# A two-layer trunk with expert retrieval: U and V rows of an expert gathered as one 8 KB row

## The reference, cut to what matters

```python
def peer(h, w_query, sub_keys, expert_u, expert_v):     # per block of 128 tokens
    qry = (x_blk @ w_query).reshape(T, 8, 2, 128)
    scores = einsum('thpd,hpnd->thpn', qry, sub_keys)   # 8 heads, 2 halves, 128 sub-keys
    top_s, top_i = top_k(scores, 16)
    ...                                                 # 16 x 16 sums, best 16 -> idx, gate
    gate = softmax(best_s)
    u = expert_u[idx]                                   # 128 picks per token, 1024 values each
    act = gelu(einsum('thkd,td->thk', u, x_blk))
    vsel = expert_v[idx]
    return einsum('thk,thkd->td', gate * act, vsel)
```

## Time and profile before

| | before |
|---|---|
| timed runs, median | 1703.7 us (1703.4 to 1704.94) |
| profiled execution, span (its own time) | 1706.2 us |
| PE busy | 1410.3 us, 83% |
| VectorE (DVE) busy | 965.0 us, 57% |
| ScalarE (ACT) busy | 379.5 us, 22% |
| POOL busy | 1095.4 us, 64% |
| moved by DMA | 619.36 MB, mean 363 GB/s |
| mean granted TensorE clock | 0.956 |

### The profile page before, as it was taken

The page is one execution under the profiler, slowest core; times in us unless marked ns, Lnnn a source line. Parts: engine busy times, 40 slices in busy tenths (PEclk is TensorE's granted clock), DMA queues, the critical chain, the costliest instruction groups (busy, mean ns, idle before and its releaser), DMA issues.

```text
span 1706.2 us, 14289 instructions
## 1 busy us (share of the span) xinstructions
PE 1410.3 (83%) x4185; PEld 672.0 (39%) x4185; DVE 965.0 (57%) x2457; ACT 379.5 (22%) x958; POOL 1095.4 (64%) x1044
## 2 busy tenths in 40 slices
PE   7999789877767898889997699888998667676777
PEld 6555555532222343334652244343663222222223
DVE  3126866758863533564557566585468657444441
ACT  4222211211221221442111221352212112111111
POOL 2003777777877776677667777677757666666663
PEclk9999899999997999989999999999999988999998
DMA  9318999999999999999999999999999999999996
GB/s 340 119 54 308 321 351 368 355 350 405 336 360 405 409 402 403 406 409 399 405 403 409 409 379 402 404 409 405 405 406 382 374 376 365 367 372 370 378 371 234
DMA packets 184836, 619.36 MB, mean 363 GB/s; under 512 B 18420, under 2 KB 18456, under 8 KB 184760
## 3 DMA queue, kind: packets, MB, share of 16 engines
q0 software_dynamic: 151184, 551.68, 83.8%
q1 hardware_dynamic: 33200, 66.72, 10.5%
q10 hardware_dynamic: 376, 0.05, 0.0%
HBM read 617.34 MB, written 1.05 MB: 362 GB/s over the span
## 4 chain that ended last, share of the span: by engine, by line
PE 42%; DMA 20%; POOL 16%; issue 14%; DVE 3%; another core or an unknown queue 3%; ACT 1%; ACTq 0%; SPq 0%; DVEq 0%; POOLq 0%
PE banks L540 24%; POOL arena L301 10%; DMA arena<-in_peer_v_dram,hnT 10%; PE banks L420 5%; POOL raw L301 4%; DMA work<-in_peer_v_dram,hnT 4%; PE banks L564 3%; PE banks L513 3%; DMA raw<-in_peer_u_dram,hnT 3%; DMA arena<-in_peer_w_query_dram 2%; PE banks L683 2%; POOL work L301 2%; PE banks L398 2%; DMA arena<-in_peer_u_dram,hnT 1%
## 5 line engine op out<-in xcount | busy, mean ns | idle before, releaser
L540 PE MATMUL banks<-arena,hnT 128*128 128x512 f32 x1536 | 754.0, 621 | 161.2 <-DMA arena<-in_peer_v_dram,hnT 95.2
L301 POOL DMA_INDIRECT arena<-in_peer_v_dram,hnT x384 | 401.2, 1045 | 236.6 <-issue 97.3
L540 PEld LDWEIGHTS banks<-arena,hnT 128*128 128x128 f32 x1536 | 279.3, 196 | 561.8 <-issue 524.5
L301 POOL DMA_INDIRECT raw<-in_peer_u_dram,hnT x256 | 271.3, 1060 | 214.7 <-DVE hnT L1508 125.3
L1394 DVE CUSTOM_DVE_ANT_0 arena<-arena,hrows 128x1024 f32<-128x1024 f32 x192 | 234.1, 1223 | 184.9 <-DMA arena<-in_peer_u_dram,hnT 144.6
L1394 DVE CUSTOM_DVE_ANT_0 raw<-raw,hrows 128x1024 f32<-128x1024 f32 x192 | 234.5, 1223 | 162.3 <-DMA raw<-in_peer_u_dram,hnT 121.6
L301 POOL DMA_INDIRECT arena<-in_peer_u_dram,hnT x256 | 269.3, 1052 | 81.9 <-issue 77.4
L540 PE MATMUL banks<-work,hnT 128*128 128x512 f32 x512 | 262.1, 639 | 61.8 <-DMA work<-in_peer_v_dram,hnT 38.7
L901 ACT ACTIVATE hnT<-ident,hnT 128x128 f32<-128x128 f32 x512 | 171.1, 392 | 282.1 <-issue 108.2
L301 POOL DMA_INDIRECT work<-in_peer_v_dram,hnT x128 | 144.5, 1129 | 52.8 <-issue 34.8
L540 PEld LDWEIGHTS banks<-work,hnT 128*128 128x128 f32 x512 | 92.6, 200 | 189.3 <-issue 180.2
(11 more groups left out here) (214 smaller groups left out, 960.2 us busy)
## 6 DMA issues: line engine op xcount, KB each, us to landing
arena<-in_diff_w_in_dram SPq DMA_DIRECT2D x24, 1024.0 KB
arena<-in_peer_w_query_dram SPq DMA_DIRECT2D x16, 1024.0 KB
arena<-in_gla_w_in_dram POOLq DMA_DIRECT2D x5, 2048.0 KB, 24.5
arena<-in_peer_w_query_dram SPq DMA_DIRECT2D x4, 2048.0 KB, 9.1
arena<-in_diff_w_out_dram SPq DMA_DIRECT2D x8, 1024.0 KB
arena<-in_peer_v_dram,hnT POOLq DMA_INDIRECT x384
work<-in_gla_w_out_dram POOLq DMA_DIRECT2D x2, 2048.0 KB, 40.2
raw<-in_peer_u_dram,hnT POOLq DMA_INDIRECT x256
```

What stands on the lines that cost most here:

```text
L301: pool.indirect_dma_start(rows(n), None, table.rearrange("l e d -> (l e) d"), bass.IndirectOffsetOnAxis(ap=places[:, o:o + 1].bitcast(u32) ...
L540: last = nc.tensor.matmul(bank(2 * (tile % NT) + half), diags[:, n % BUFS * P:(n % BUFS + 1) * P], v_rows(n)[:, half * 512:(half + 1) * 51 ...
```

## The change

U and V of each layer are laid side by side as `peer_uv` (rows of 8 KB), so one gather brings both rows of a pick. The 16 buffers of 4 KB become 8 "pair" buffers of 8 KB for the first 128 picks and 9 afterwards (`homes`). A buffer is reused when the sum of its last pick is done (`BEFORE`, `v_used`). The lag of 16 picks is gone, and layer 1 begins 14 ticks earlier. GELU, weights and diagonals of a group are made together on ScalarE, in groups of 2 picks, and of 4 during the attention of layer 1 (`groups`); the weights, formerly one VectorE instruction for 8 picks, are now one ScalarE instruction for each pick. The sub-keys come as `peer_keys_t`, already turned, so that the transposes and their copies go. In the diff below the long index expressions of ScalarE's operands are shortened to names.

```diff
-GRP = 8
-BUFS = 8
+DIAGS = 8
-BASE = (148, 276)
-FINAL = 430
+BASE = (134, 262)
+FINAL = 414
+AHEAD = 7
+TICKS = ROWS + LANDED + 4
-ADD_T, HN2_T = (11, 15), 17
-QUERY_T, QUERY_TICKS = {3: 20, 4: 32, 5: 44, 6: 56, 7: 68}, 10
+ADD_T, HN2_T = (8, 10), 12
+QUERY_T, QUERY_TICKS = {2: 10, 3: 22, 4: 38, 5: 56, 6: 74, 7: 90}, 14
...
+def groups():
+    out, n = [], 0
+    while n < ROWS:
+        narrow = all(not b + ATT_T - 2 <= n + LANDED < b + NORM_O + 2 for b in BASE)
+        size = 2 if narrow or n % 4 else 4
+        out.append((n, size))
+        n += size
+    return out
+GROUPS = groups()
+SUM_T = [first + size + LANDED + j for first, size in GROUPS for j in range(size)]
...
+ROW = 2 * D
+EARLY = ("raw0", "raw1", 6144, 4096, "work0", "work1", "work2", "work3")
+LATE = (8192, 10240, 12288, 14336, 20480, "raw0", "raw1", 6144, 4096)
...
@@ sync
-            sp.wait_ge(S("aT_done"), NT)
-            sp.dma_start(keys..., peer_sub_keys[0].rearrange("h q n d -> n (h q) d"))
+            sp.dma_start(ar(A_KEYT, HP * P), peer_keys_t[0]).then_inc(S("keys_loaded"), 16)
@@ gpsimd
+            table = peer_uv.rearrange("l e d -> (l e) d")
+            for n in range(ROWS):
+                if n % LIST == 0:
+                    pool.wait_ge(S("listed"), n // LIST + 1)
+                if n == 3:
+                    pool.wait_ge(S("kv_done"), 3)
+                if n in (4, 6):
+                    pool.wait_ge(S("out_done"), n // 2 + 1)
+                if n == SLOTS:
+                    pool.wait_ge(S("scores_done"), 4 * NT)
+                if BEFORE[n] >= 0:
+                    pool.wait_ge(S("v_used"), BEFORE[n] + 1)
+                pool.indirect_dma_start(pair(n), None, table, ...
+                    ).then_inc(S(f"pair_loaded_{HOME[n]}"), 16)
@@ tensor: key_transposes, key1_transposes removed
-                while summed < v_at(int(t) - LANDED):
+                while summed < ROWS and SUM_T[summed] < int(t):
                     expert_sum(summed)
@@ scalar: keys_out, keys1_out removed
+            def expert_weights(g):
+                first, size = GROUPS[g]
+                o = first % PICKS
+                act.wait_ge(S("u_dotted"), first + size)
+                A(acts[:, o:o + size], dots[:, o:o + size], ACT.Gelu).then_inc(S("gelu_done"), 1)
+                act.wait_ge(S("settled"), first // LIST + 1)
+                act.wait_ge(S("gelu_done"), g + 1)
+                for n in range(first, first + size):
+                    A(weights[n], acts[n], ACT.Copy, scale=gate[n]).then_inc(S("weighted"), 1)
+                for n in range(first, first + size):
+                    ...
+                    if n >= DIAGS:
+                        act.wait_ge(S("v_used"), n - DIAGS + 1)
+                    act.wait_ge(S("weighted"), n + 1)
+                    A(diags[n % DIAGS], ident[:], ACT.Copy, scale=weights[n]).then_inc(S("diag_ready"), 1)
@@ vector
-            def weigh(g): ...
-                latest = START[tile] + b * LIST - 1
+                latest = START[tile] + b * LIST - AHEAD
```

More of the change, by code:

```diff
@@ L116, in trunk_kernel @@
                  diff_w_in, lq1, lk1, lq2, lk2, diff_norm, diff_w_out,
-                 peer_w_query, peer_sub_keys, peer_u, peer_v, out):
+                 peer_w_query, peer_keys_t, peer_uv, out):
     f32, f32r, bf16 = mybir.dt.float32, mybir.dt.float32r, mybir.dt.bfloat16
@@ L168, in trunk_kernel @@
         words = hnT[:].rearrange("p m k t -> p (m k t)")
-        dots, acts, weights, places, diags = (words[:, o:o + n] for o, n in (
-            (0, PICKS), (PICKS, PICKS), (2 * PICKS, PICKS), (3 * PICKS, PICKS), (4 * PICKS, BUFS * P)))
+        dots, acts, weights, places = (words[:, k * PICKS:(k + 1) * PICKS] for k in range(4))
+        diags = g_e3
         def x1(unit, off=0, n=D):
@@ L297, in _ @@
             pool.memset(causalT[0:GCH, GCH:P], 0.0).then_inc(S("const"), 1)
-            def gather(table, n, rows, loaded):
+            table = peer_uv.rearrange("l e d -> (l e) d")
+            for n in range(ROWS):
+                if n % LIST == 0:
[8 more added lines that the diff above has]
+                    pool.wait_ge(S("v_used"), BEFORE[n] + 1)
                 o = n % PICKS
                 pool.indirect_dma_start(
-                    rows(n), None, table.rearrange("l e d -> (l e) d"),
+                    pair(n), None, table,
                     bass.IndirectOffsetOnAxis(ap=places[:, o:o + 1].bitcast(u32), axis=0)
[L304 to L324, removed]
+                    ).then_inc(S(f"pair_loaded_{HOME[n]}"), 16)
         @block.tensor
@@ L332, in _ @@
                                 ).then_inc(S("gains_transposed"), 1)
[L334 to L349, removed]
             def hx_transposes():
@@ L910, in at @@
                         raised += 1
-                    while acted < u_at(ticks - LANDED) // GRP:
-                        expert_act(acted)
+                    while acted < len(GROUPS) and sum(GROUPS[acted]) - 1 + LANDED <= ticks:
+                        expert_weights(acted)
                         acted += 1
-                    while diagonals < v_at(ticks):
-                        diagonal(diagonals)
-                        diagonals += 1
                     ticks += 1
@@ L1035, in _ @@
             v_out(3)
-            for n in range(1, 4):
-                keys_out(n)
             act.preload_act_table(ACT.Silu)
@@ L1421, in at @@
                         settled += 1
-                    while ticks >= WEIGH_FIRST and weighed < u_at(ticks - LANDED - 2) // GRP:
-                        weigh(weighed)
-                        weighed += 1
                     ticks += 1
@@ L1562, in _ @@
             search(1, 1)
+            search(1, 2)
+            at(ANGLES_T)
             angles()
```

167 lines of the change are left out of this document (73 added, 94 removed).

## The result

| | time, median of the runs | ratio to before, 95% interval |
|---|---|---|
| before | 1703.55 us (1701.17 to 1704.94, 4 runs) | |
| after | 1641.64 us (1638.84 to 1647.24, 4 runs) | 0.9639 [0.9615, 0.9663] |

The account below looks back on a forecast made before the run. Bound: transfers at about 410 GB/s where saturated, POOL's descriptor writing elsewhere. Terms -40 - 6 - 37 - 5 + 4 + 8 = -76 gave 1630 us profiled, 1628 timed; range 1592 to 1685.

Parts of the forecast that it names:

- POOL sets the pace of the gather-only stretches: 200 to 500 and 1300 to 1650 us: descriptor writing limits the gathers; one gather a pick gains 40 and 37 us.
- A gather of 8 KB rows costs POOL what one of 4 KB rows did: POOL, each pick: 0.94 + 0.30 = 1.24 us for the single gather, at the upper end 2.2 us.
- the row length buys nothing and POOL pays double: Rival, all gathers: 8 KB rows stay at 409 GB/s and cost POOL 2.2 us a pick; 1664 us, chance 0.14.
- The rate of 8 KB rows: Gather transfers: between 409 and 420 GB/s, taken as 415, 2.53 us for a pick.
- The start: From the first gather at 140 us: later pairs wait for output projections, DMA idle about 152 to 162; plus 4 us.
- The last stretch: The end, after 1650 us: 14.9 MB at 415 GB/s take 36 us, closing chain 6.2 us; minus 5 us.
- 500 to 1300 us: -6, and +8 for hold and hand-overs: Layer 1: longer rows gain 6 us; buffers held until the sum, and hand-overs, cost 8 (ends 0 and +40).
- The prediction's own sign of being wrong: Layer 1: slices falling under 400 GB/s would show the forecast wrong.
- the transfers are saturated already, and only the row length can help: 500 to 1300 us, at 403 GB/s: 71% of the bytes 1.4% faster, minus 8, part given back, minus 6.
- long hold eats the gain in layer 1: Rival, 500 to 1300 us: holding buffers until the sum costs +40 in place of +8; 1662 us, chance 0.14.
- The spare time of 6.6 us: Pair buffers, groups of 2: slack left before a reused buffer's gather must start; hardly 1.6 us in attention groups of 4.
- Slower, the loop as bound: Rival, everywhere: the loop of a pair buffer takes 28 us, 3.11 us a pick; +36, 1740 us, chance 0.11.

Follow-up runs that it names:

- the two 4 KB gathers: Changed kernel, but each pick again as two gathers of 4 KB rows, U then V, into its pair buffer: 1744.3 us, ratio 1.0202.
- the last version: Changed kernel with layer-1 weights in 8 KB rows, groups of 2 in the attention and ScalarE's angle part seven ticks later: 1607.2 us, ratio 0.9436.

## Why the prediction was right, and where it was off

*POOL sets the pace of the gather-only stretches.* Right, and shown by the two 4 KB gathers. -36 and -41 measured, -40 and -37 forecast. That the queue of gathers carries the DMA engines over a stop shows in after itself:

```profile
1389.50 0.94 POOL L331 DMA_INDIRECT arena<-in_peer_uv_dram,hnT  x1 [6.69 <-PE banks L533]
```

No window of 3 us from 1376 to 1400 moves less than 418 GB/s. Before, a stop of 3.45 us was followed by a wait of 3.29 us for the row.

*A gather of 8 KB rows costs POOL what one of 4 KB rows did.* Right: 1.06 to 1.12 us as a mean by memory, 0.94 undisturbed, plus 0.30. POOL's busy time is 559.9 for 532 operations, 1095.4 for 1044 before. The rival "the row length buys nothing and POOL pays double" is refuted in both halves.

*The rate of 8 KB rows.* The upper end held: 8 ns fixed for a row gave 420, the taken value was 415, and the steady rate is 421. This gave 4 us more than forecast from 1300 to 1650 us. The 8 ns go with the row and not with the packet: the packets of the 2 KB rows were 3.6 KB as a mean, nearly as large as a 4 KB row, and still moved 390 against 409 GB/s. In the timeline of after the dots are 2.48 us apart, each after waiting for its row, where the undisturbed dot of the earlier trace rows stood behind an "issue" and so didn't show what paced it:

```profile
1400.70 1.22 DVE L1378 CUSTOM_DVE_ANT_0 arena<-arena,banks 128x1024 f32<-128x1024 f32 x1 [1.25 <-DMA arena<-in_peer_uv_dram,hnT]
...
1403.18 1.22 DVE L1378 CUSTOM_DVE_ANT_0 arena<-arena,banks 128x1024 f32<-128x1024 f32 x1 [1.26 <-DMA arena<-in_peer_uv_dram,hnT]
```

The rows travel whole: the queue of the gathers moves 551.65 MB in 77456 packets, 7.1 KB each as a mean, POOL's shorter rows of GLA weights among them. Before it had 151184; the difference, 73728, is 65536 for the rows that were joined and 16 for each of the 512 gathers saved. The Trainium skill's page "DMA: Bandwidth & Descriptors", section "Why small descriptors are slow (HBM only)", gives 3 cycles of overhead a packet; an estimate from that and the 850 MHz of its section "Where 436 GB/s comes from" would have been 414, and the measured rate is above it.

*The start.* Right in its mechanism, wrong in its price: +4 forecast, nothing measured at 200 us. The first eight gathers of after are issued where the blocks of the output projection let them:

```profile
143.77 0.94 POOL L331 DMA_INDIRECT arena<-in_peer_uv_dram,hnT  x1 [0.30 <-issue]
164.32 0.94 POOL L331 DMA_INDIRECT work<-in_peer_uv_dram,hnT  x1 [19.60 <-PE banks L413]
...
171.18 0.94 POOL L331 DMA_INDIRECT work<-in_peer_uv_dram,hnT  x1 [4.69 <-PE banks L413]
```

164.5 and 171.4 were forecast. The DMA engines stand still as forecast, 2 GB/s from 160 to 165 us, but before was slow here too, 217 and 228 GB/s from 165 to 175 us. The last stretch was right to the microsecond, and so was its chain: the last row's dot starts at 1631.01 and the last sum ends at 1637.11, 6.1 us, where 6.2 were counted.

*500 to 1300 us: -6, and +8 for hold and hand-overs.* This is the mis-sized term: +2 forecast, +21 measured. These 19 us, less the 4 that the rate gave from 1300 to 1650 us, are the 15 by which the forecast of -76 missed the measured -61. Its first half was even better than taken: undisturbed, this stretch rose from 405 to 412 GB/s (560 to 640 us), 1.7% of 800 us, -14. The second half, the stops, cost some +35 instead of +8. The prediction's own sign of being wrong came true here: eight of the twenty slices of layer 1 are under 400 GB/s. Its error is in the step "the transfers are saturated already, and only the row length can help": it asked what the longer gather rows do for the gathers, and not what they do to SP's 2 KB rows beside them. The issues of SP from 560 to 640 us show the landing times (KB each, median us to landing), of after and of the last version:

```profile
arena<-in_diff_w_in_dram SPq DMA_DIRECT2D x4, 1024.0 KB, 39.9
arena<-in_diff_w_out_dram SPq DMA_DIRECT2D x4, 1024.0 KB, 31.0
```

```profile
arena<-in_layer_w_dram SPq DMA_DIRECT2D x8, 1024.0 KB, 9.4
```

Halving the number of the weights' rows (4 KB) takes 43.7 us of PE's waits to 5.1, and two 4 KB gathers for a pick leave 6.4 with the weights as they were; so it is short rows beside long ones that come late. That the queues share the engines by turns, one row each, would explain it but was not looked at directly, and a gather queue that is now always full goes along with the longer rows in all these kernels.

*The rival "long hold eats the gain in layer 1"* had the place right and nearly the size of the stops (+40 priced, some +35 measured; its total of 1662 lacks the better rate). The hold alone isn't what decides, since one buffer less changes nothing and weights in rows of 8 KB take away more than half of the dips from 500 to 1300 us (42.9 to 18.3). But of the 18.3 that are left, nearly all lie in the attention, where the rival looked for them. The spare time of 6.6 us a buffer was not left over either: a deeper queue took it up. In layer 0 a gather of after lands 13.0 us after its issue (median), where 5.1 were counted. Long holds matter in that PE's waits now reach POOL: a gather needs the sum 9 picks back, some 22 us, so a PE stop of 9 us with slow matmuls behind it is passed on whole.

*Slower, the loop as bound.* Didn't come: POOL waits 0.8 to 2.3 us for a sum at each pick, while rows issued earlier keep the DMA engines busy. Its price was also added up wrong: 13.6 us (groups of 2), 4 ticks and another tick and a half are 27.4 us, the break-even, and not 28. The kernel with two 4 KB gathers comes to 1744.3, near the 1740 priced, but there POOL took part in it, so the agreement is luck.

## What to carry to other kernels

When a descriptor-writing engine is within a few per cent of the transfer rate, halving its operations is worth far more than the longer rows: it lets the queue fill up again. When the rows of one queue are made longer, look at every other queue beside it: rows that stay short arrive later, and the engine that needs them hands its wait on to the gathers. Lay weights so that a partition's part is one long row; here it cost no work on the chip and gave 28 us.

## What the runs showed of the hardware

Rows of 8 KB from HBM, each to one partition, travel as one packet, at 421 GB/s; 4 KB rows give 411 in saturated windows. Two gathers for a pick keep POOL busy 2.1 us, one of 8 KB rows 1.1. The fixed part of 8 ns a row, worked out from 2 KB and 4 KB rows, foretold it to 1 GB/s. With 8 KB gathers beside them, weights in rows of 2, 4 and 8 KB give 412, 418 and 421 GB/s over the same 80 us. After an idle time of PE of 9 us the granted clock was at 0.50, the 1.2 GHz level, for about the next 6 us, in which a pick's sum took 3.62 us instead of 1.88, so that each stop cost more than its own length.
